# Two more expert blocks loaded during the routing, into rooms that serve once

## What is computed

```python
def hier_moe(h, w_group, b_group, w_expert, b_expert, w_gate_e, w_up_e, w_down_e):
    ...
    grp = jnp.argmax(g_logits, axis=-1)
    ...
    top_v, top_i = lax.top_k(e_in, EXPERT_TOPK)                  # 2 experts of 32 for each token
    weight = p_grp[:, None] * jax.nn.softmax(top_v, axis=-1)
    ...
    def expert_block(args):
        xb, e = args                                             # the rows of one expert
        return (jax.nn.silu(xb @ w_gate_e[e]) * (xb @ w_up_e[e])) @ w_down_e[e]
    ...
    y = jnp.zeros((N, D), h.dtype).at[tok[order]].add(y_slot)    # back to the tokens
```

## Time and profile before

| what | value |
|---|---|
| median of 3 runs | 2889.88 us (2889.05 to 2892.0) |
| the profiled execution's own time | 2890.03 us |
| its span, first to last instruction | 2888.2 us |
| PE, DVE, ACT, POOL busy | 97%, 61%, 22%, 10% |
| bytes read from and written to the chip's memory | 337.79 MB and 14.16 MB |
| mean granted clock of PE | 0.994 of full speed |

### The profile page before, as it was taken

One profiled execution on the slowest core, in us unless ns is written; L12 is line 12 of the kernel. 1 busy time (PEld: TensorE's weight loads), 2 busy tenths in 40 slices (PEclk: granted clock), 3 DMA queues, 4 the chain that ended last, 5 costly groups with the idle time before them and its releaser, 6 DMA issues.

```text
span 2888.2 us, 34140 instructions
## 1 busy us (share of the span) xinstructions
PE 2800.1 (97%) x13374; PEld 2144.1 (74%) x13374; DVE 1769.7 (61%) x3747; ACT 623.5 (22%) x1359; POOL 299.3 (10%) x285
## 2 busy tenths in 40 slices
PE   9999999999999999999999899999999999999985
PEld 6888887668888877888864587888877766885321
DVE  4788697775766466566358766677356445664222
ACT  1322120022221021221022412222022464001001
POOL 0000020020000100000101430000100373001110
PEclk9999999999999999999999999999999999999998
DMA  4323333112313222132211111232212201257997
GB/s 170 117 102 124 128 124 110 59 61 93 117 75 115 88 88 88 59 117 102 102 62 59 44 59 66 88 117 94 96 73 95 103 16 59 88 225 287 424 425 321
DMA packets 61333, 349.50 MB, mean 121 GB/s; under 512 B 8560, under 2 KB 14832, under 8 KB 22384
## 3 DMA queue, kind: packets, MB, share of 16 engines
q1 hardware_dynamic: 44640, 320.88, 28.9%
q10 hardware_dynamic: 11920, 17.98, 1.8%
q0 software_dynamic: 4608, 8.40, 0.8%
HBM read 337.79 MB, written 14.16 MB: 122 GB/s over the span
## 4 chain that ended last, share of the span: by engine, by line
PE 89%; DVE 4%; DMA 3%; SPq 2%; ACT 1%; issue 1%; POOL 0%; ACTq 0%; DVEq 0%; POOLq 0%
PE bank L922 33%; PE bank L1120 31%; PE bank L538 6%; PE bank L547 5%; SPq L3863 2%; PE bank L3924 2%; DMA ring<-in_weights 2%; PE bank L2773 2%; PE bank L576 2%; PE bank L3358 2%; PE bank L2757 1%; PE bank L3943 1%; PE bank L568 1%; PE bank L671 0%; PE bank L2995 0%
## 5 line engine op out<-in xcount | busy, mean ns | idle before, releaser
L922 PE MATMUL bank<-area,mixed 128*128 128x256 f32 x2264 | 508.4, 379 | 2.4 <-DVE mixed L944 1.8
L922 PEld LDWEIGHTS bank<-area,mixed 128*128 128x128 f32 x2264 | 429.6, 190 | 62.1 <-DVE mixed L944 2.5
L922 PE MATMUL bank<-area,ring 128*128 128x256 f32 x1536 | 346.3, 379 | 0.1
L1120 PE MATMUL bank<-area 128*128 128x256 f32 x1440 | 323.9, 379 | 0.0
L922 PEld LDWEIGHTS bank<-area,ring 128*128 128x128 f32 x1536 | 291.4, 190 | 40.3 <-DVE area L963 0.5
L1120 PEld LDWEIGHTS bank<-area 128*128 128x128 f32 x1440 | 273.6, 190 | 37.2
L1120 PE MATMUL bank<-buf_b,area 128*128 128x256 f32 x1040 | 239.3, 379 | 0.0
L1120 PE MATMUL bank<-buf_a,area 128*128 128x256 f32 x1040 | 239.1, 379 | 0.0
L1120 PEld LDWEIGHTS bank<-buf_b,area 128*128 128x128 f32 x1040 | 197.5, 190 | 27.1 <-issue 0.3
L1120 PEld LDWEIGHTS bank<-buf_a,area 128*128 128x128 f32 x1040 | 197.6, 190 | 26.9
L944 DVE TENSOR_TENSOR mixed<-ring 128x512 f32<-128x512 f32 (+2 forms) x95 | 63.9, 673 | 225.1 <-PE bank L922 224.8
(11 more groups left out here) (637 smaller groups left out, 4292.6 us busy)
## 6 DMA issues: line engine op xcount, KB each, us to landing
ring<-in_weights SPq DMA_DIRECT2D x236, 1024.0 KB, 4.8
area<-in_weights SPq DMA_DIRECT2D x35, 1024.0 KB, 27.5
buf_b<-in_weights SPq DMA_DIRECT2D x10, 1024.0 KB, 26.1
buf_a<-in_weights SPq DMA_DIRECT2D x8, 1024.0 KB, 24.8
const<-in_weights SPq DMA_DIRECT2D x5, 1024.0 KB, 27.7
norm<-in_weights SPq DMA_DIRECT2D x4, 1024.0 KB, 23.0
mixed<-in_weights SPq DMA_DIRECT2D x4, 1024.0 KB, 26.3
area<-area ACTq DMA_DIRECT2D x20, 128.0 KB, 2.4
```

What stands on the lines that cost most here:

```text
L922: mm = pe.e.matmul(b, w[:, k * P:(k + 1) * P], x(INPUT_OF[p], unit.lo + k), start=(unit.key, BANK_OF[p]) not in begun, stop=unit.last and ...
L1120: mm = pe.e.matmul(out[:, half * H:(half + 1) * H], weights[:, at:at + P], x(name, d), start=fresh and half == 0 and d == 0, stop=half == ...
```

## The change

Two rooms are added to `HOMES`, called `ONCE`: region 6144 (for block 0) and region 4096 (for block 2). They lie where `xt` was, and where `e_hidden`, `e_turned`, `rows_in[3]` and `rows_out` will be, so each serves for one block only. The first pass over the rooms thus has 22 blocks, and 20 rooms go on in turn. `sync_first_experts` loads the same 17 rooms at the same waits as before (now blocks 1 and 3 to 18), and then blocks 0 and 2, right behind `norm`. `sync_slots` starts at block 19. `block_ahead` says whose reader a load waits for: block 22 waits for block 1's, block 23 for block 3's, 24 for 4's and so on.

`xt` moves into the rooms of `xs_turned` and of `rows_in[1]` and `rows_in[2]`. These two can be cleared only once the tokens are stored, so POOL now clears one room during the routing, and the others one by one between the gathers. The fourth clearing, and with it gather 3, waits for up 0, which reads block 0 out of that room.

The other edits belong to the branch that isn't taken.

```diff
-    xt = [region(4096 + b * D, D) for b in range(TB)]
+    xt = [region(at, D) for at in (12288, 15360, 17408, 18432)]
...
-    COMMON = IN_RING[:1] + EARLY + MERGE + IN_RING[RING - 1:] + IN_RING[1:RING - 1] + [(norm[:, :], pos_loaded, 1)]
+    ONCE = [(region(6144, BLOCK), once_loaded[0], 0), (region(4096, BLOCK), once_loaded[1], 0)]
+    ONCE_AT = (0, 2)
+    COMMON = ONCE[:1] + IN_RING[:1] + ONCE[1:] + EARLY + MERGE + IN_RING[RING - 1:] + IN_RING[1:RING - 1] + [(norm[:, :], pos_loaded, 1)]
...
     def home(block, homes):
-        turn, at = divmod(block - FIRST, len(homes))
-        where, loaded, earlier = homes[at]
-        return where, loaded, 16 * (earlier + turn + 1)
+        k = block - FIRST
+        if k < len(homes):
+            where, loaded, earlier = homes[k]
+            return where, loaded, 16 * (earlier + 1)
+        turn, at = divmod(k - len(homes), len(homes) - len(ONCE))
+        where, loaded, earlier = homes[kept(homes)[at]]
+        return where, loaded, 16 * (earlier + turn + 2)
+
+    def kept(homes):
+        return [k for k in range(len(homes)) if k not in ONCE_AT]
+
+    def block_ahead(block, homes):
+        k, n = block - FIRST - len(homes), len(homes) - len(ONCE)
+        return FIRST + kept(homes)[k] if k < n else block - n
...
+        sy.wait_ge(*g.done(("squares", "nsa")))
+        for k in (len(COMMON) - 1,) + ONCE_AT:
             load_home(sy, FIRST + k, COMMON)
...
             elif k >= len(HOMES):
-                sy.wait_ge(tensor_groups, gs.reader[block - len(HOMES)])
+                sy.wait_ge(tensor_groups, gs.reader[block_ahead(block, HOMES)])
...
         po.wait_ge(both_ready, 1)
-        for i in range(3):
-            po.e.memset(rows_in[i], 0.0).then_inc(rows_cleared, 1)
+        po.e.memset(rows_in[0], 0.0).then_inc(rows_cleared, 1)
...
         po.wait_ge(tokens_stored, 16 * TB)
-        po.wait_ge(rows_cleared, 3)
         po.wait_ge(slotted, 1)
-        for p in range(3):
+        for p in range(4):
+            if p == 3:
+                po.wait_ge(*gs.done(("up", 0)))
+            if p:
+                po.e.memset(rows_in[p], 0.0).then_inc(rows_cleared, 1)
+            po.wait_ge(rows_cleared, p + 1)
             bring(p)
-        po.e.memset(rows_in[3], 0.0).then_inc(rows_cleared, 1)
-        po.wait_ge(rows_cleared, 4)
-        bring(3)
```

More of the change, by code:

```diff
@@ L3817, in build_in @@
     xs_done, e_silu, e_mul, rows_copied, summed = sem("xs_done"), sem("e_silu"), sem("e_mul"), sem("rows_copied"), sem("summed")
+    once_loaded = [sem(f"once{i}") for i in range(2)]
     turned_back, slots_weighted = sem("turned_back"), sem("slots_weighted")
@@ L3865, in sync_first_experts @@
     def sync_first_experts(sy):
[L3867 to L3880, removed]
+        early = [k for k in kept(COMMON) if k < len(COMMON) - 1]
+        sy.wait_ge(tensor_groups, g.reader[FIRST - RING])
+        load_home(sy, FIRST + early[0], COMMON)
+        for way in ("ga", "gb", "pa", "pb"):
+            sy.wait_ge(*g.done((("square", "b", way, KD // 2 - 1), 0, PARTS[-1])))
+        for k in early[1:1 + len(EARLY)]:
+            load_home(sy, FIRST + k, COMMON)
+        sy.wait_ge(*b_mixed("mix", KD // 2 - 1))
+        for k in early[1 + len(EARLY):1 + len(EARLY + MERGE)]:
+            load_home(sy, FIRST + k, COMMON)
+        sy.wait_ge(router_scaled, 2)
+        for n, k in enumerate(early[1 + len(EARLY + MERGE):]):
+            if n:
+                sy.wait_ge(tensor_groups, g.reader[FIRST + n - RING])
+            load_home(sy, FIRST + k, COMMON)
+        sy.wait_ge(*g.done(("squares", "nsa")))
+        for k in (len(COMMON) - 1,) + ONCE_AT:
             load_home(sy, FIRST + k, COMMON)
@@ L4132, in sync_all @@
         block = FIRST + len(COMMON)
+        sy.wait_ge(*ga.done(("eu", 0, 1)))
         for e in range(NEXP):
@@ L4136, in sync_all @@
             sy.e.dma_start(a_weights[e % 4], combine_dram[e:e + 1, :].to_broadcast([P, T])).then_inc(landed[e % 4], 16)
-            while block < n_blocks and ga.reader[block - len(COMMON)] <= ga.index["ed", e, KD - 1]:
-                sy.wait_ge(tensor_groups, ga.reader[block - len(COMMON)])
+            while block < n_blocks and ga.reader[block_ahead(block, COMMON)] <= ga.index["ed", e, KD - 1]:
+                sy.wait_ge(tensor_groups, ga.reader[block_ahead(block, COMMON)])
                 load_home(sy, block, COMMON)
@@ L4148, in scalar_all @@
         ac.wait_ge(tokens_stored, 16 * TB)
-        ac.e.dma_start(a_gain, io["gain"]).then_inc(gain_loaded, 16)
         for e in range(NEXP):
@@ L4152, in scalar_all @@
                 ac.wait_ge(*ga.done(("eg", e, m)))
+                if e == 1 and m == 0:
+                    ac.e.dma_start(a_gain, io["gain"]).then_inc(gain_loaded, 16)
                 if e > 1:
@@ L4165, in vector_all @@
     def vector_all(ve, ga, r):
-        ve.wait_ge(rows_cleared, 3)
+        ve.wait_ge(rows_cleared, 1)
+        ve.wait_ge(tokens_stored, 16 * TB)
         vector_scaled(ve, "nsa", r, h_all, "ffn_g", ga)
```

## The result

The change makes the kernel slower by a little: 2894.44 us (median of 22 runs, 2891.87 to 2895.7) against 2890.07 us before (22 runs, 2889.05 to 2893.11), a ratio of 1.0014 with a 95% interval of 1.0008 to 1.002. The profiled execution of after took 2895.2 us, its span is 2893.4 us, 5.2 us more than before.

A forecast was written before the change was run, and what follows sets the result against it. PE bounds the kernel nearly everywhere, but DMA transfers set the end. 2.3 us of backlog saved less 1.2 us for the late first gather gives 1.1 us: 2888.9 us against the profiled 2890.03, 2888.8 as median; range 2885.0 to 2892.2.

The forecast's parts named there:

- The bound and the rooms: Last stretch: transfers set the end, but block 24 and later loads wait for up 1's end before and after the change.
- the hole: DMA engines run out of loads and idle some 3 us before up 1's end, near 2657.
- 5.0 us: Gain if two blocks simply left the full stretch; the whole gain coming through was a rival, 2884.9 us, chance 0.12.
- The backlog saved: DMA queue at up 1's end: block 24 lands 4.7 instead of 7.0 us after issue, saving at most 2.3 us.
- the price of the two loads among the stores: During the routing: blocks and token stores share the DMA engines, first gather 1.2 us later, bounds 0 to 3.2.
- the full stretch: 2640 to the last load, DMA engines full without a break; its 421 GB/s was used for blocks and stores together.
- the lower bound: Blocks and stores together move at no more than the stores' 350 GB/s: 12.0 us, last store at 2635.5.
- PE's clock: Rival: PE idles before turn 0, up 0 starts at 1.2 GHz, 1.7 us added; 2892.6 us; 0.13 with other late waits.
- its trigger: The clock falls from a first-gather delay of about 2.3 us, a PE idle of 2.8 us.
- The cover of POOL's new order: Clearing rooms between the gathers costs nothing; gather 1 has 1.7 us of cover.

The follow-up runs named there:

- room_less2: The kernel before with 18 rooms instead of 20 (second half of buf_a and mixed are no rooms): 2893.29 us, 1.0012 of before.
- split: The change with block 0 loaded ahead of the token stores on SP's queue and block 2 behind them on ACT's: 2888.67 us, 0.9995 of before.
- one_block: The change with only block 0 loaded ahead during the routing, instead of two blocks: 2888.61 us, 0.9995 of before.
- split_silu: split with ACT's table for Silu loaded ahead, out of the path between up 0 and up 1: 2887.15 us, 0.9991 of before.
- no_loads: The change's token place and POOL order alone, without rooms that serve once or blocks loaded ahead: 2890.45 us, 1.0 of before.
- behind_stores: The change with both loads issued by ACT on its own queue, behind its four token stores: 2890.17 us, 0.9999 of before.
- silu_before: The kernel before with ACT's table for Silu loaded ahead of the experts by one activation without use: 2889.36 us, 0.9997 of before.
- silu_one: one_block with ACT's table for Silu loaded ahead by one activation without use: 2888.68 us, 0.9994 of before.

## Why the prediction was wrong

Forecast were 2888.8 us, a small gain, in a range of 2885.0 to 2892.2; measured were 2894.44 us, a small loss. By its steps:

- **The bound and the rooms: right.** The end hangs on up 1's end, the hole is where it was forecast, and loading two blocks ahead does not bring 5.0 us. Shown by the windows, by room_less2, by split against one_block, and by split_silu.
- **The backlog saved: right in kind, its size not settled.** 2.3 us were taken from two landings, and block 24 now lands 4.8 us after its issue instead of 7.0, as forecast; its row of the kernel after:

```profile
area<-in_weights SPq DMA_DIRECT2D x1, 1024.0 KB, 4.8
```

  The last load's distance from up 1's end shrank by only 0.86 us in this pair of executions, but the one of before is the shortest without a hole: from no_loads to split, whose up 1 ends at the same place (37.59 us), the rest of the span shrinks by 3.0 us. By the medians it is 1.0 us in split, and 2.4 us after the change if its up 1 is 6.75 us late in most executions (6.75 - 4.37). The forecast's 2.3 lies among these.
- **The step that failed: the price of the two loads among the stores.** The text has "4.2 MB at 421 GB/s are 10.0 us", a last store at 2633.5, and so a first gather 1.2 us late, at most 3.2. Measured: 4.38 us. Two things were wrong in it. The sum took the rate of the full stretch, but 2624 to 2630 ran at 295 GB/s, below even the 350 of the lower bound; and the transfers ended raggedly, while the gather waits for the last store's last packet:

```profile
2634.00:2636.00 2.00, 2.00 (x38) 1.89 (x35) 0.17 (x1) 0.00 (x0) 0.00 (x0) 1.00 0.12 45
```

  Against 421 GB/s the first loses 1.8 us (6 x (1 - 295/421)) and the second 1.8 us (2 x (1 - 45/421)): as an estimate, together 3.6 us, where 3.2 us (4.38 - 1.2) were missing. In one_block, where the stores simply follow the block, the delay was 1.2 us and covered.
- **PE's clock:** it was listed as a rival at 0.13, with its trigger (a gather 2.3 us late or more), its place and its price (1.7 us). With the gather 4.4 us late it came true: 1.70 us in up 0, and 0.53 us ahead of it that the rival left out. The price has a like in the trace of the kernel before: the four windows of 1 us from 2189.70 were granted 0.54, 0.50, 0.50 and 0.76, which together lose 1.7 us. The trigger does not hold: in behind_stores the clock fell behind an idle of 1.82 us, with the gather landing 1.3 us late.
- **The cover of POOL's new order: right** (no_loads: the first gather on the table, the median as before).

With the measured terms the forecast's own sum reads +4.38 + 0.14 + 2.23 - 0.86 = 5.9 us on the profiled execution, less the 0.66 us by which its stage began sooner.

What stays open: why the loads' packets took nearly twice as long while stores stood behind them, and why the transfers ended raggedly. The second block delays the last store by 5.0 us (8.8 against 3.8 us to landing) though its bytes are 2.5 us; the slower loads and the ragged end are where that time lies, but their cause wasn't tried apart.

## What to carry to other kernels

A room or a prefetch ahead of a bound stage is worth only what the stage's first hard wait lets through: find the first load that still waits for the same event, and read the backlog there. A stretch in which the DMA engines look half-empty may hold transfers that somebody waits for: load ahead of them only as much as their cover allows, and put the rest behind them. An engine that waits longer may also run slower afterwards, so a late transfer can cost more than its delay.

## What the runs showed of the hardware

- No byte of the stores on ACT's queue moved for 4.3 us after the first one's issue, while loads issued earlier on SP's queue kept the DMA engines busy at 100.0% (2622.7 to 2627 after the change).
- In the same stretch the loads fell from 0.43 to 0.22 MB in a microsecond at an unchanged busy share.
- PE's clock also fell where nothing was late, and in some executions only. The windows below show it ahead of turn 0 in no_loads (POOL's new order) and in silu_before (the old order) at 0.50 during matmuls without use, and in split_silu (the new order) at 1.00. PE's idle times just ahead were 1.55 and 0.37 us in no_loads and 1.54 and 0.38 us in split_silu. one_block, silu_one and split show the fall too; before and room_less2 do not. It makes up 0 start 0.63 us later in no_loads than before, and the same 0.6 us stand in the table for the others.

```profile
2630.00:2633.00 3.00, 3.00 (x15) 3.00 (x16) 1.75 (x10) 0.00 (x0) 2.01 (x2) 0.50 0.05 12
2630.00:2633.00 3.00, 2.97 (x14) 2.98 (x15) 1.94 (x12) 1.37 (x2) 1.52 (x2) 0.50 0.01 3
2630.00:2633.00 3.00, 2.46 (x31) 2.16 (x27) 2.21 (x13) 1.49 (x2) 1.11 (x1) 1.00 0.81 328
```
